# Whole-expert weight loads and a reordered expert loop in a two-block transformer kernel

## The chip, the cores and the metric

One Trainium2 chip, of which the kernel uses one core. The metric is device time in microseconds (us) for one execution. Everything is float32. TensorE (PE) multiplies, with its weight load shown apart as PEld; ScalarE is ACT, VectorE is DVE, GpSimd is POOL, SyncE is SP and issues most of the transfers.

## What is computed

Two models run one after the other on 256 tokens of width 1024. The first is two layers of attention, convolution and MLP. The second has two layers as well, and each of its layers ends in a mixture of experts. That is the part the change touches. Each token chooses one of four groups of experts and two of the eight experts in it:

```python
def _hier_moe(h, w_r1, b_r1, w_r2, b_r2, w_gate, w_up, w_down):
    ...
    eid = grp[:, None] * MOE_PER_GROUP + top_i
    combine = jnp.einsum('tk,tke->te', w_sel, jax.nn.one_hot(eid, MOE_EXPERTS, dtype=jnp.float32))

    def expert_step(acc, xs):
        wg, wu, wd, gcol = xs
        y = (jax.nn.silu(t @ wg) * (t @ wu)) @ wd
        return acc + y.astype(jnp.float32) * gcol[:, None], None
```

There are 32 experts per layer, each with three matrices of 1024 x 512 or 512 x 1024 (2 MB each, 6 MB per expert). The result of each expert is weighted and added into the tokens that chose it.

## The kernel before

The engines run programs written out by hand, and semaphores order them. All weights come from the chip's memory. Outside the experts they come in chunks of 2 MB (`CW` = 4096 floats in each of 128 partitions) into a ring of four slots (`ring`, `RING` = 4).

The expert stage is `moe(i)`, once per layer. After routing, it runs rounds (one round here: each expert gets at most 64 of the 256 tokens, `SLOTS`), and a round is eight **turns** of four experts (`TURNS`, `GROUP_OF`). In a turn:

- DVE builds `place` (which token goes to which slot) and `weighted` for four experts.
- PE **gathers** the tokens of all four experts at once (`gather`, 16 products of 128 x 256 into four PSUM banks), and ACT copies the four banks to `gathered`.
- Then for each of the four experts: `gate_up` (16 products, 128 x 512, which use two of the expert's three chunks), ACT's silu, DVE's product (`hidden`), `turn` (four transposes on PE, to bank 1), ACT's copy to `turned`, `down` (8 products with the third chunk) and DVE's copy to `y`. `spread` (8 products that add y to the tokens in the four `sums` banks) of an expert comes one expert later, between the next `gate_up` and the next `turn`. For the fourth expert it comes at the end of the turn.

On SP, `load_experts` issues a chunk as soon as the chunk four places earlier has been used: a third of an expert at a time, gated by `up_done` (the end of `gate_up`) or `down_done` (the end of `down`). So several transfers are in flight at most times:

```python
if t == 0:
    sp.wait_ge(S.sem(f"moe{i}_down_done"), it * 4 + (e + 1))
else:
    sp.wait_ge(S.sem(f"moe{i}_up_done"), it * 4 + (e + 2))
...
sp.dma_start(ring[:, q % RING, :], src).then_inc(S.sem(f"moe{i}_landed{q % RING}"), 16)
```

In the traces a float32 product is two matmul instructions, so `gate_up` shows as x32, `down`, `spread` and a quarter of a gather as x16, x16 and x8, `turn` as x4. Lines: L965 `gate_up`, L987 `down`, L996 `spread`, L494 `turn`, L473 `gather` (a helper that other stages use too), L1301 ACT's copy of gathered tokens, L1305 silu, L1307 ACT's copy to `turned`, L1964 `hidden`, L1967 the copy to `y`, L393 the issue of an expert chunk, L1011 the closing of `sums`.

Of the kernel before, what the change touches and what calls it, by code (L numbers as in the profile page):

```python
# [23 lines left out]
P = 128  # L24
T = 256
# [213 lines left out]
def two_blocks_kernel(nc, stream, experts, tokens, ctx_tokens, params, consts, consts2, pool_counts, positions,  # L239
                      na_bias, out, counted):  # L240
    stack = ExitStack()
    with stack:
# [37 lines left out]
        def carve(tensor, spec):  # L280
            at, views = 0, {}
            for name, *dims in spec:
                n = int(np.prod(dims))
                v = tensor[:, at:at + n]
                if len(dims) > 1:
# [24 lines left out]
                         ("weighted", 2, GROUP_OF * 2 * SLOTS), ("turned", 512), ("y", 512), ("silu", T), ("hidden", T)])  # L310
# [56 lines left out]
        def _(sp):  # L367
# [10 lines left out]
            def load_experts(i):  # L378

                S.wait(sp, "chunk_used", C_POOL - 1 if i == 0 else C_POOL)  # L380

                def turn(it, turn_no):
                    for q in range(EXPERT_CHUNKS * GROUP_OF):
                        e, t = q // EXPERT_CHUNKS, q % EXPERT_CHUNKS


                        if t == 0:
                            sp.wait_ge(S.sem(f"moe{i}_down_done"), it * 4 + (e + 1))
                        else:
                            sp.wait_ge(S.sem(f"moe{i}_up_done"), it * 4 + (e + 2))  # L390
                        n = i * EXPERTS * EXPERT_CHUNKS + q
                        src = experts[bass.ds(turn_no * 12 + n, 1), :, :].rearrange("a p c -> p (a c)")
                        sp.dma_start(ring[:, q % RING, :], src).then_inc(S.sem(f"moe{i}_landed{q % RING}"), 16)  # L393


                turn(0, 0)
# [38 lines left out]
        def _(pool):  # L435
# [6 lines left out]
            for i in range(2):  # L442
                for j, kind in enumerate(("down_done", "down_done", "up_done", "up_done")):
                    pool.memset(small[:, 120 + 4 * i + j:121 + 4 * i + j], 0.0).then_inc(S.sem(f"moe{i}_{kind}"), 1)

# [6 lines left out]
            S.wait(pool, "x_normed", "post", 0, 0)  # L452
# [6 lines left out]
        def _(pe):  # L459
# [450 lines left out]
            def moe(i):  # L910
# [29 lines left out]
                def landed(it, q):  # L940

                    raised(f"landed{q % RING}", it, 16 * (q // RING + 1), 48)
                    return ring[:, q % RING, :]

                def gather(it):

                    raised("placed", it, 1, 1)
                    for j in range(4):
                        bank = banks[3 - j]
                        for a in range(2):  # L950
                            k = 2 * j + a
                            mm = product(bank[:, a * T:(a + 1) * T],
                                         [(M["by_token"][:, t, k * P:(k + 1) * P], M["place"][:, t, :]) for t in range(2)])
                        give(mm, "gather_done")

                def gate_up(it, e):
# [3 lines left out]
                    for c in range(2):  # L960
                        w = landed(it, 3 * e + c).rearrange("p (k c) -> p k c", k=4)
                        for kk in range(4):
                            k = 4 * c + kk
                            for half in range(2):
                                mm = pe.matmul(banks[0][64 * half:64 * half + 64, :],  # L965
                                               M["gathered"][:, k, e * SLOTS:(e + 1) * SLOTS],
                                               w[:, kk, 512 * half:512 * half + 512], start=(k == 0), stop=(k == KT - 1))
                    give(mm, "up_done")

                def turn(it, e):  # L970
# [4 lines left out]
                    for t in range(2):  # L975
                        mm = transposed(banks[1][:, T + t * P:T + (t + 1) * P],
                                        M["weighted"][:, t, 2 * e * SLOTS:2 * (e + 1) * SLOTS])
                    give(mm, "turn_done")

                def down(it, e):  # L980

                    raised("turned", it, e + 1, 4)
                    w = landed(it, 3 * e + 2).rearrange("p (k c) -> p k c", k=4)
                    for k in range(4):
                        hT = M["turned"][:, (k % 2) * P + (k // 2) * 64:(k % 2) * P + (k // 2) * 64 + 64]
                        for half in range(2):
                            mm = pe.matmul(banks[2][64 * half:64 * half + 64, :], hT, w[:, k, 512 * half:512 * half + 512],  # L987
                                           start=(k == 0), stop=(k == 3))
                    give(mm, "down_done")

                def spread(it, e):

                    raised("y_kept", it, e + 1, 4)
                    for m in (0, 4, 1, 5, 2, 6, 3, 7):
                        a, c = 64 * (m // 4), (m % 4) * P
                        pe.matmul(sums[m // 2][:, (m % 2) * T:(m % 2 + 1) * T], M["y"][a:a + 64, c:c + P],  # L996
                                  M["turned"][a:a + 64, T:2 * T], start=False, stop=False, skip_group_check=True)

                with pe.Fori(0, rounds_of(pe, i)) as rnd:
                    with pe.Fori(0, TURNS) as g:  # L1000
                        it = rnd * TURNS + g
# [34 lines left out]
        def _(act):  # L1036
# [249 lines left out]
            def moe(i):  # L1286
# [9 lines left out]
                with act.Fori(0, rounds_of(act, i)) as rnd:  # L1296
                    with act.Fori(0, TURNS) as g:
                        it = rnd * TURNS + g
                        for j in range(4):
# [877 lines left out]
```

## Time and profile before

| | |
|---|---|
| device time, median of 3 runs | 2636.77 us (2635.98 to 2636.89) |
| the profiled execution, first to last instruction | 2643.5 us |
| PE busy | 2364.3 us (89%) |
| DVE, ACT busy | 909.9 us (34%), 480.3 us (18%) |
| read from memory | 619.08 MB, of which 192 expert chunks of 2 MB |
| expert stage of layer 0, first `gate_up` to the last `spread` | 1461.20 to 1979.42 us |
| expert stage of layer 1, the same | 2089.20 to 2607.08 us |

The profiled execution is read from the trace of one run, with times from its first instruction. The page gives for each engine its busy time; the chain of work is followed back from the last instruction to what released each step. PE counted as busy need not be PE at its peak, and a queue's time from issue to landing holds the waiting behind other transfers.

### The profile page before, as it was taken

The page shows a single profiled execution, that of the slowest core. Times are in us where ns is not written, and L with a number is a line of the kernel's source. Part 1 is how long each engine was busy: PE and PEld are TensorE (multiplying, and loading weights), DVE is VectorE, ACT ScalarE, POOL GpSimd, SP SyncE. Part 2 cuts the span into 40 slices and gives each one's busy share as a digit, 9 for nine tenths or more (in the row PEclk, how much of TensorE's full clock was granted, in tenths as well). Part 3 has the DMA queues.
Part 4 walks back from the last instruction along what each step waited for, and adds up shares of the span by engine and source line. Part 5 has one row for each costly group of instructions (what it writes and reads, how often), then busy time and mean ns, then how long its engine had stood idle before and what let it go on. Part 6 is the DMA issues. An engine that isn't in the chain of part 4 may idle for free.

```text
span 2643.5 us, 30301 instructions
## 1 busy us (share of the span) xinstructions
PE 2364.3 (89%) x12616; PEld 1594.5 (60%) x12616; DVE 909.9 (34%) x2001; ACT 480.3 (18%) x784; POOL 4.1 (0%) x20
## 2 busy tenths in 40 slices
PE   7999989989999899989887899999995799999996
PEld 6766779988767699946765344444433444444443
DVE  7889345541473365420364000000007300001002
ACT  1113113311221143210130111111110111111110
POOL 0000000000000000000000000000000000000000
PEclk9989999999999999999988999999997899999998
DMA  6335624534446434522003789999972399999993
GB/s 249 139 128 224 253 96 182 199 127 159 190 166 249 159 128 176 208 85 96 32 1 135 324 377 385 383 384 385 385 298 104 164 379 385 384 385 386 382 384 144
DMA packets 43320, 621.13 MB, mean 235 GB/s; under 512 B 4816, under 2 KB 4816, under 8 KB 5232
## 3 DMA queue, kind: packets, MB, share of 16 engines
q1 hardware_dynamic: 42624, 615.76, 57.1%
q0 software_dynamic: 624, 4.39, 0.4%
q8 instruction: 48, 0.79, 0.1%
q14 instruction: 24, 0.20, 0.0%
HBM read 619.08 MB, written 1.05 MB: 235 GB/s over the span
## 4 chain that ended last, share of the span: by engine, by line
PE 77%; DVE 11%; DMA 7%; ACT 3%; issue 1%; DVEq 0%; SPq 0%; ACTq 0%
PE bank L473 32%; PE bank L965 15%; DMA ring<-in_experts 7%; PE bank L987 6%; PE sums L996 3%; PE bank L656 2%; PE bank L657 2%; PE bank L658 2%; PE sums L658 2%; PE sums L657 2%; PE sums L656 2%; PE bank L494 2%; PE bank L483 2%; PE sums L717 2%; DVE wide L1433 1%; DVE arena L1460 1%
## 5 line engine op out<-in xcount | busy, mean ns | idle before, releaser
L965 PE MATMUL bank<-ring,wide 128*64 128x512 f32 x2048 | 455.2, 594 | 21.3 <-ACT wide L1301 12.2
L473 PE MATMUL bank<-h,ring 128*128 128x256 f32 x1920 | 440.1, 392 | 23.8 <-DVE h L1358 12.1
L473 PEld LDWEIGHTS bank<-h,ring 128*128 128x128 f32 x1920 | 375.2, 197 | 87.6 <-DVE h L1358 12.9
L965 PEld LDWEIGHTS bank<-ring,wide 128*64 128x64 f32 x2048 | 145.6, 137 | 314.9 <-issue 281.1
L987 PE MATMUL bank<-ring,wide 128*64 128x512 f32 x1024 | 233.8, 598 | 45.2 <-ACT wide L1307 45.2
L1964 DVE TENSOR_TENSOR wide<-bank,wide 128x256 f32<-128x256 f32 x64 | 27.2, 425 | 578.4 <-ACT wide L1305 578.4
L1660 DVE TENSOR_TENSOR ring_split<-ring,arena_split 128x2048 fp32r<-128x2048 f32 x64 | 143.8, 2288 | 110.6 <-ACT arena_split L1186 110.4
L473 PE MATMUL bank<-arena,ring 128*128 128x256 f32 x624 | 147.0, 398 | 31.9 <-DVE arena L1996 19.8
L1967 DVE COPY wide<-bank 128x512 f32<-128x512 f32 x64 | 44.3, 692 | 371.4 <-PE bank L987 371.4
L987 PEld LDWEIGHTS bank<-ring,wide 128*64 128x64 f32 x1024 | 68.3, 136 | 169.5 <-issue 125.1
L656 PE MATMUL bank<-h_split,arena_split 128*128 128x256 f32 x512 | 146.8, 287 | 15.0 <-DVE ring_split L1660 15.0
L473 PEld LDWEIGHTS bank<-arena,ring 128*128 128x128 f32 x624 | 124.2, 200 | 53.3 <-issue 15.5
L657 PE MATMUL bank<-scratch_split,arena_split 128*128 128x256 f32 x512 | 146.4, 286 | 0.0
L658 PE MATMUL bank<-h_split,ring_split 128*128 128x256 f32 x512 | 146.2, 286 | 0.0
L656 PE MATMUL sums<-smax_split,arena_split 128*128 128x256 f32 x512 | 144.9, 283 | 0.0
L657 PE MATMUL sums<-smax_split,arena_split 128*128 128x256 f32 x512 | 144.9, 283 | 0.0
L658 PE MATMUL sums<-smax_split,ring_split 128*128 128x256 f32 x512 | 144.9, 283 | 0.0
L1186 ACT ACTIVATE arena_split<-ring 128x2048 fp32r<-128x2048 f32 x64 | 118.9, 1906 | 113.3 <-PE sums L658 113.3
L996 PE MATMUL sums<-wide 64*128 64x256 f32 x1024 | 127.9, 389 | 12.7 <-DVE wide L1967 12.7
L996 PEld LDWEIGHTS sums<-wide 64*128 64x128 f32 x1024 | 93.6, 186 | 74.3 <-issue 38.9
L1305 ACT ACTIVATE wide<-bank 128x256 f32<-128x256 f32 x64 | 24.6, 384 | 619.4 <-PE bank L965 619.4
L473 PE MATMUL bank<-wide 128*128 128x256 f32 x528 | 124.3, 394 | 7.5 <-DVE wide L1952 7.5
(265 smaller groups left out, 2604.6 us busy)
## 6 DMA issues: line engine op xcount, KB each, us to landing
ring<-in_experts SPq DMA_DIRECT2D x192, 2048.0 KB, 12.4
ring<-in_stream SPq DMA_DIRECT2D x100, 2048.0 KB, 7.6
wide<-in_na_bias POOLq DMA_DIRECT2D x1, 1536.0 KB, 11.9
arena<-in_consts POOLq DMA_DIRECT2D x1, 1088.0 KB, 8.8
x<-in_tokens SPq DMA_DIRECT2D x1, 1024.0 KB, 6.2
scratch<-in_ctx_tokens POOLq DMA_DIRECT2D x1, 1024.0 KB, 5.0
out_x<-x SPq DMA_DIRECT2D x1, 1024.0 KB, 3.9
par<-in_params SPq DMA_DIRECT2D x1, 715.0 KB, 7.5
```

The costliest lines, as they stand in the source:

```text
L473: mm = pe.matmul(dst, a, b, start=(first and i == 0), stop=(i == len(terms) - 1))
L483: mm = pe.matmul(bank[:, 0:T], ones, src(0, q), start=(q == 0), stop=(q == tiles[0] - 1))
L494: return pe.transpose(dst, src, ident)
L656: pe.matmul(dst, w_hi, v_hi, start=start, stop=False, skip_group_check=True)
L657: pe.matmul(dst, w_hi, v_lo, start=False, stop=False, skip_group_check=True)
L658: return pe.matmul(dst, w_lo, v_hi, start=False, stop=stop, skip_group_check=True)
L717: mm = pe.matmul(sums[c % 2][g:g + 32, :], cond[:, k, :], w[:, k, :], start=(k < 4), stop=(k >= 4))
L965: mm = pe.matmul(banks[0][64 * half:64 * half + 64, :], M["gathered"][:, k, e * SLOTS:(e + 1) * SLOTS], w[:, kk, 512 * half:512 * half + 5 ...
L987: mm = pe.matmul(banks[2][64 * half:64 * half + 64, :], hT, w[:, k, 512 * half:512 * half + 512], start=(k == 0), stop=(k == 3))
L996: pe.matmul(sums[m // 2][:, (m % 2) * T:(m % 2 + 1) * T], M["y"][a:a + 64, c:c + P], M["turned"][a:a + 64, T:2 * T], start=False, stop=Fal ...
L1186: act.activation(HI[("up", "down")[part]][:, j % 2, :], ring[:, slot, 2048 * part:2048 * part + 2048], ACT.Copy).then_inc(S.sem("mlp_high" ...
L1660: dve.tensor_tensor(split["ring"][:, slot, 2048 * part:2048 * part + 2048], v, HI[("up", "down")[part]][:, j % 2, :].bitcast(F32), ALU.sub ...
```

## The change

The same products are computed. What differs:

1. **Weights.** An expert's three chunks lie side by side in memory (48 KB in each partition) and come in one transfer of 6 MB. There are two whole-expert buffers: the first three ring slots, and the first 12,288 columns of `arena`, a work area that is idle in the expert stages. The transfer of expert e waits until `down` of expert e-2 is done. The first two of a stage go out ahead.
2. **Order on PE.** The gather for the next turn is cut into four pieces, one in each expert, between `gate_up` and `turn`; only a round's first gather stands alone. Everything that belongs to gathered tokens has two buffers (`gathered`, `placed_at`, `weighted_at`; the second ones lie in `h` and `scratch`). `spread` of the previous expert moves from before `turn` to between `turn` and `down`, `turned` has two halves, and the first spread of a stage adds zeros. The loop over turns runs over pairs of turns, three times, and the last two turns are written out.
3. **ACT and DVE.** DVE instead of ACT copies the gathered tokens. DVE clears one half of `turned` and `y` ahead of the rounds.
4. **POOL.** The load of `pool_counts` (512 KB, into `arena`) waits for the end of layer 0's experts. Eight small memsets are gone.

```diff
             def load_experts(i):
-                S.wait(sp, "chunk_used", C_POOL - 1 if i == 0 else C_POOL)
-                def turn(it, turn_no):
-                    for q in range(EXPERT_CHUNKS * GROUP_OF):
-                        e, t = q // EXPERT_CHUNKS, q % EXPERT_CHUNKS
...
+                def turn(it, turn_no, first=False):
+                    for e in range(GROUP_OF):
+                        if first and i and e == 1:
+                            S.wait(sp, "chunk_used", C_POOL)
+                        if not first or e >= 2:
+                            sp.wait_ge(S.sem(f"moe{i}_down_done"), it * 4 + (e - 1))
+                        src = experts[bass.ds(turn_no * 4 + (i * EXPERTS + e), 1), :, :].rearrange("a p c -> p (a c)")
+                        sp.dma_start(expert_slots[e % 2], src).then_inc(S.sem(f"moe{i}_landed{e % 2}"), 16)
...
-            S.wait(pool, "x_normed", "post", 0, 0)
+            S.wait(pool, "moe_summed", 0)
             pool.dma_start(PL["counts"], pool_counts.rearrange("p (a b) -> p a b", a=4))\
...
-                        gather(it)
-                        for e in range(GROUP_OF):
-                            gate_up(it, e)
-                            if e:
-                                spread(it, e - 1)
-                            turn(it, e)
-                            down(it, e)
-                        spread(it, GROUP_OF - 1)
+                def experts_of(it, buf, last=False):
+                    for e in range(GROUP_OF):
+                        gate_up(it, e, buf)
+                        if not last:
+                            if e == 0:
+                                raised("placed", it, 2, 1)
+                            raised("gather_kept", it, 4 + e, 4)
+                            gather(1 - buf, e, banks[3])
+                        turn(it, e, buf)
+                        raised("y_kept", it, e + 1, 4)
+                        spread((e + 1) % 2)
+                        down(it, e)
...
-                        for j in range(4):
-                            act.wait_ge(S.sem(f"moe{i}_gather_done"), it * 4 + (j + 1))
-                            act.activation(flat2(M["gathered"][:, 2 * j:2 * j + 2, :]), banks[3 - j][:, :], ACT.Copy)\
-                               .then_inc(S.sem(f"moe{i}_gather_kept"), 1)
...
+                def keep_gathered(it, j, buf, bank):
+                    dve.wait_ge(S.sem(f"moe{i}_gather_done"), it * 4 + (j + 1))
+                    dve.tensor_copy(flat2(gathered[buf][:, 2 * j:2 * j + 2, :]), bank[:, :])\
+                       .then_inc(S.sem(f"moe{i}_gather_kept"), 1)
...
+                        dve.wait_ge(S.sem(f"moe{i}_silued"), it * 4 + (e + 1))
+                        dve.tensor_tensor(M["hidden"], banks[0][:, T:2 * T], M["silu"], ALU.mult)\
+                           .then_inc(S.sem(f"moe{i}_hidden"), 1)
+                        if not last:
+                            keep_gathered(it + 1, e, 1 - buf, banks[3])
+                        dve.wait_ge(S.sem(f"moe{i}_down_done"), it * 4 + (e + 1))
+                        dve.tensor_copy(M["y"], banks[2][:, :]).then_inc(S.sem(f"moe{i}_y_kept"), 1)
...
+                dve.memset(M["turned"][:, 1, :], 0.0)
+                dve.memset(M["y"], 0.0).then_inc(S.sem(f"moe{i}_y_kept"), 1)
```

**PE, two experts in the middle of a turn of layer 0.** The rows give line, operation, what is written and read, the shape, and the semaphores waited for. Before (L965 `gate_up`, L996 `spread`, L494 `turn`, L987 `down`; "landed" is the arrival of a chunk):

```order
L965 MATMUL bank<-ring,wide 64x512 [waits moe0_landed3]
L965 MATMUL bank<-ring,wide 64x512 x7
L935 REGISTER_ALU
L965 MATMUL bank<-ring,wide 64x512 [waits moe0_landed0]
L965 MATMUL bank<-ring,wide 64x512 x7
L996 MATMUL sums<-wide 128x256 [waits moe0_y_kept]
L996 MATMUL sums<-wide 128x256 x7
L935 REGISTER_ALU
L494 MATMUL bank<-con,wide 128x128 [waits moe0_hidden]
L494 MATMUL bank<-con,wide 128x128 x3
L987 MATMUL bank<-ring,wide 64x512 [waits moe0_landed1,moe0_turned]
L987 MATMUL bank<-ring,wide 64x512 x7
```

and of the changed kernel (L959 `gate_up`, L470 a piece of the gather, L491 `turn`, L989 `spread`, L981 `down`; "landed0" and "landed1" are the two whole-expert buffers):

```order
L959 MATMUL bank<-arena,wide 64x512 [waits moe0_landed1]
L959 MATMUL bank<-arena,wide 64x512 x7
L932 REGISTER_ALU
L470 MATMUL bank<-scratch,wide 128x256 [waits moe0_gather_kept]
L470 MATMUL bank<-scratch,wide 128x256 x3
L932 REGISTER_ALU
L491 MATMUL bank<-con,wide 128x128 [waits moe0_hidden]
L491 MATMUL bank<-con,wide 128x128 x3
L989 MATMUL sums<-wide 128x256 [waits moe0_y_kept]
L989 MATMUL sums<-wide 128x256 x7
L981 MATMUL bank<-arena,wide 64x512 [waits moe0_landed1,moe0_turned]
L981 MATMUL bank<-arena,wide 64x512 x7
```

A quarter of a gather now stands between `gate_up` and `turn`, `spread` stands between `turn` and `down`, and the wait of `down` for its own chunk is gone: what `gate_up` waited for holds all three matrices.

**SP, the first turn of layer 0's experts.** Before, 12 transfers, of which some wait for `up_done`:

```order
L376 DMA ring<-in_stream 128x4096 [waits filled] x5
L393 DMA ring<-in_experts 128x4096 [waits moe0_down_done,filled]
L393 DMA ring<-in_experts 128x4096 [waits moe0_up_done] x2
L393 DMA ring<-in_experts 128x4096 [waits moe0_down_done]
L393 DMA ring<-in_experts 128x4096 [waits moe0_up_done] x2
```

and of the changed kernel, 4 transfers:

```order
L382 DMA ring<-in_stream 128x4096 [waits filled] x5
L393 DMA ring<-in_experts 128x12288 [waits filled]
L393 DMA arena<-in_experts 128x12288
L393 DMA ring<-in_experts 128x12288 [waits moe0_down_done]
L393 DMA arena<-in_experts 128x12288 [waits moe0_down_done]
```

The first two have no wait for an expert, and each later one waits for `down_done` alone. No transfer starts at an `up_done` any more.

## Rows read from the trace of the kernel before

**Rows 1.** The page: the span, and the chain that ended last, by engine.

```profile
span 2643.5 us, 30301 instructions
...
PE 77%; DVE 11%; DMA 7%; ACT 3%; issue 1%; DVEq 0%; SPq 0%; ACTq 0%
```

**Rows 2.** Stretches: us, busy of PE, PEld, DVE, ACT, POOL, PEclk, DMA share, GB/s.

```profile
1461.20:1979.42 518.22, 471.71 (x2401) 209.18 (x2401) 49.55 (x93) 68.53 (x108) 0.00 (x0) 1.00 0.89 372
2089.20:2607.08 517.88, 471.73 (x2401) 209.36 (x2401) 49.56 (x93) 68.53 (x108) 0.00 (x0) 1.00 0.89 373
1585.44:1651.17 65.73, 59.82 (x306) 26.89 (x305) 6.43 (x13) 8.88 (x14) 0.00 (x0) 1.00 0.92 385
1470.00:1500.00 30.00, 27.32 (x142) 10.82 (x144) 2.23 (x4) 2.47 (x5) 0.00 (x0) 1.00 0.99 421
```

**Rows 3.** The chain in order of time, one turn: start us, us, what.

```profile
1585.44 7.12 PE bank L473 x32
...
1593.31 7.11 PE bank L965 x32
...
1606.33 6.87 PE bank L965 x32
1613.20 1.93 PE sums L996 x16
...
1620.05 6.89 PE bank L965 x32
...
1627.11 10.72 DMA ring<-in_experts
1637.83 0.04 issue
```

**Rows 4.** ACT in order of time, gathered copies: start us, us, what, idle before.

```profile
1587.40 0.60 ACT L1301 ACTIVATE wide<-bank 128x512 f32<-128x512 f32 x1 [7.16 <-PE bank L473]
1589.13 0.60 ACT L1301 ACTIVATE wide<-bank 128x512 f32<-128x512 f32 x1 [1.13 <-PE bank L473]
```

**Rows 5.** PE and SP in order of time: a `down`, the issue it releases.

```profile
1550.99 3.65 PE L987 MATMUL bank<-ring,wide 128*64 128x512 f32 x16 [0.69 <-ACT wide L1307]
...
1554.83 0.33 SPq L393 DMA_DIRECT2D ring<-in_experts  x1
```

**Rows 6.** Tiles `in_experts` (three issues by themselves), then `in_stream`: ns, starts, landing.

```profile
L393 SPq DMA_DIRECT2D ring<-in_experts x1: 327/327/327, 1406.4 to 1406.4; - x1
...
DMA to landing us min/median/max: 7.7/7.7/7.7
...
L393 SPq DMA_DIRECT2D ring<-in_experts x1: 676/676/676, 1407.7 to 1407.7; - x1
...
DMA to landing us min/median/max: 21.1/21.1/21.1
...
L393 SPq DMA_DIRECT2D ring<-in_experts x1: 328/328/328, 1468.3 to 1468.3; - x1
...
DMA to landing us min/median/max: 9.0/9.0/9.0
...
DMA to landing us min/median/max: 7.3/7.6/24.9
```

**Rows 7.** The chain: first `gate_up` of the last turn, in each stage.

```profile
1921.54 7.11 PE bank L965 x32
...
2549.00 7.11 PE bank L965 x32
```

**Rows 8.** DVE ahead of the first turn, and its memset by line: start, us.

```profile
1449.75 0.76 DVE L1952 TENSOR_TENSOR wide<-con,smax 128x256 f32<-128x256 f32 x2 [1.38 <-issue]
...
L1415 DVE MEMSET wide<- x1: 1765/1765/1765, 29.1 to 29.1; 128x2048 f32 x1
```

**Rows 9.** DMA issues (KB, us to landing), and DVE's first work in `arena` afterwards.

```profile
arena<-in_pool_counts POOLq DMA_DIRECT2D x1, 512.0 KB, 3.4
...
2013.95 0.29 DVE L1984 COPY arena<-h 128x256 f32<-128x256 f32 x1
```

More of the change, by code:

```diff
@@ L378, in load_experts @@
             def load_experts(i):
-                S.wait(sp, "chunk_used", C_POOL - 1 if i == 0 else C_POOL)
-                def turn(it, turn_no):
-                    for q in range(EXPERT_CHUNKS * GROUP_OF):
-                        e, t = q // EXPERT_CHUNKS, q % EXPERT_CHUNKS
[L387 to L396, printed above, removed]
+                def turn(it, turn_no, first=False):
[6 more added lines that the diff above has]
+                        sp.dma_start(expert_slots[e % 2], src).then_inc(S.sem(f"moe{i}_landed{e % 2}"), 16)
+                if i == 0:
+                    S.wait(sp, "chunk_used", C_POOL - 1)
+                turn(0, 0, first=True)
                 with sp.Fori(1, TURNS) as g:
@@ L938, in give, with landed, gather, gate_up @@
                     ins.then_inc(S.sem(f"moe{i}_{kind}"), 1)
[L940 to L947, printed above, removed]
-                    for j in range(4):
[L949 to L956, printed above, removed]
+                def landed(it, e, c):
+                    raised(f"landed{e % 2}", it, 16 * (e // 2 + 1), 32)
+                    return expert_slots[e % 2][:, c * CW:(c + 1) * CW]
+                def gather(buf, j, bank):
+                    for a in range(2):
+                        k = 2 * j + a
+                        mm = product(bank[:, a * T:(a + 1) * T],
+                                     [(M["by_token"][:, t, k * P:(k + 1) * P], placed_at[buf][:, t, :]) for t in range(2)])
+                    give(mm, "gather_done")
+                def gate_up(it, e, buf):
                     if e == 0:
@@ L960, in gate_up @@
                     for c in range(2):
-                        w = landed(it, 3 * e + c).rearrange("p (k c) -> p k c", k=4)
+                        w = landed(it, e, c).rearrange("p (k c) -> p k c", k=4)
                         for kk in range(4):
@@ L996, in spread @@
                         pe.matmul(sums[m // 2][:, (m % 2) * T:(m % 2 + 1) * T], M["y"][a:a + 64, c:c + P],
[L997 to L1001, printed above, removed]
-                        gather(it)
-                        for e in range(GROUP_OF):
-                            gate_up(it, e)
-                            if e:
-                                spread(it, e - 1)
-                            turn(it, e)
-                            down(it, e)
-                        spread(it, GROUP_OF - 1)
+                                  M["turned"][a:a + 64, before, T:2 * T], start=False, stop=False, skip_group_check=True)
+                def experts_of(it, buf, last=False):
[10 more added lines that the diff above has]
+                        down(it, e)
+                rounds = rounds_of(pe, i)
+                with pe.Fori(0, rounds) as rnd:
+                    raised("placed", rnd, 1, TURNS)
+                    for j in range(4):
+                        gather(0, j, banks[3 - j])
+                    with pe.Fori(0, TURNS // 2 - 1) as g:
+                        for b in range(2):
+                            experts_of(rnd * TURNS + g * 2 + b, b)
+                    experts_of(rnd * TURNS + (TURNS - 2), 0)
+                    experts_of(rnd * TURNS + (TURNS - 1), 1, last=True)
+                pe.wait_ge(S.sem(f"moe{i}_y_kept"), rounds * EXPERTS + 1)
+                spread(1)
                 for b in range(4):
@@ new lines, in moe @@
+                dve.memset(M["turned"][:, 1, :], 0.0)
+                dve.memset(M["y"], 0.0).then_inc(S.sem(f"moe{i}_y_kept"), 1)
+                with dve.Fori(0, rounds_of(dve, i)) as rnd:
+                    place(rnd * TURNS, 0, 0)
+                    for j in range(4):
+                        keep_gathered(rnd * TURNS, j, 0, banks[3 - j])
+                    with dve.Fori(0, TURNS // 2 - 1) as g:
+                        for b in range(2):
+                            experts_of(rnd * TURNS + g * 2 + b, g * 2 + b, b)
+                    experts_of(rnd * TURNS + (TURNS - 2), TURNS - 2, 0)
+                    experts_of(rnd * TURNS + (TURNS - 1), TURNS - 1, 1, last=True)
@@ L2095, in pack_experts @@
     out[:, :, 2] = a["moe_w_down_2"].reshape(2, EXPERTS, 4, P, D).transpose(0, 1, 3, 2, 4).reshape(2, EXPERTS, P, CW)
-    return out.reshape(2 * EXPERTS * EXPERT_CHUNKS, P, CW)
+    return out.transpose(0, 1, 3, 2, 4).reshape(2 * EXPERTS, P, EXPERT_CHUNKS * CW)
 def pack_params(a):
```

73 lines of the change are left out of this document (36 added, 37 removed).

## The prediction

> **What bounds the kernel now.** I read the page's span and chain first: PE holds 77% of the chain and transfers 7% [rows 1]. The change acts in the two expert stages alone, so I cut those out: 518.2 and 517.9 us, each at a granted clock of 1.00, with the transfers 0.89 busy and 372 to 373 GB/s [rows 2]. Both PE and memory are near their limit there, and the question is how they interlock. One turn takes 65.7 us at 385 GB/s, while a stretch in which chunks stood in the queue without a break moved 421 GB/s at a share of 0.99 [rows 2]. So transfers pause within a turn. The chain shows where: through the gather and the first `gate_up` PE leads, and late in the turn 10.7 us of a chunk's transfer are on the chain [rows 3]. All four slots stay full while PE gathers (7.12 us), no transfer runs, and the turn's last expert pays with a short wait. PE would have been ready for that chunk at 1620.05 + 13.72 (an expert, below) + 3.4 (half of 6.87) = 1637.2, and it landed at 1637.8 [rows 3]: PE alone needs only some 0.7 us less per turn. So hiding the gather from PE is worth something only if the transfers keep pace. That decides the case.
>
> **What the change does to PE.** From one `gate_up` to the next within a turn it is 13.72 us (1606.33 to 1620.05) [rows 3]: `gate_up`, `spread`, `turn`, a wait of 0.69 us for ACT's copy [rows 5], `down`. The new order adds a quarter of the gather, 1.73 us by the distance of two of ACT's copies [rows 4]. It puts `spread` (1.93 us [rows 3]) behind `turn`, which covers the 0.69 us of ACT. The quarter of the gather in turn covers silu and `hidden`, as `spread` did. That is 13.72 + 1.73 - 0.69 = 14.76 us, and 0.2 us more (7.11 against 6.87, less the part that is only the end of the last product [rows 3]) where `gate_up` starts after a wait: 14.96. Four experts are 59 to 60 us of PE per turn. If nothing else counted, a turn would lose 6 us.
>
> **What it does to the transfers.** A buffer is refilled only when its whole expert is done, so one buffer runs in a cycle: expert on PE, issue, transfer of 6 MB, next expert but one. The terms are 14.96 us of PE; 0.18 us from the end of `down` (1554.64) to SP's issue (1554.83) [rows 5]; the transfer T; 0.04 us from landing to PE [rows 3]. No row shows a transfer of 6 MB. The nearest are the four chunks issued back to back into an idle queue: the first, issued at 1406.4, landed after 7.7 us, the fourth, issued at 1407.7, after 21.1 [rows 6]. That is 14.7 us for three more, 4.9 us each, and three chunks, the same 6 MB, land 7.7 + 2 x 4.9 = 17.5 us after the first issue. I take T = 17.5. From below I bound it by the fastest chunk into an idle queue, 7.3 us, which gives 17.1; from above by the slowest of the expert chunks that met an idle queue, 9.0 us, which gives 18.8 [rows 6]. I stay near 17.5 since that is the same number of bytes from the same tensor.
>
> The cycle is 14.96 + 0.18 + 17.5 + 0.04 = 32.68 us for two experts, so 65.4 us per turn, against 65.7 of the one shown. The gather's 7 us vanish from PE's own sum, and a wait for a landing of about 3 us in every second expert takes their place. The fixed part of a transfer (7.7 - 4.9 = 2.8 us) was exposed once per turn, when the queue restarted after the gather; now it is exposed in each buffer's cycle.
>
> **The sum, per stage.** Seven turns at 65.36 are 457.5 us. The last turn has no gather left to hide, so a start after a wait costs 13.02 (first expert of a turn, 1593.31 to 1606.33 [rows 3]) - 0.69 + 1.93 = 14.26 us on PE. To the third expert: 14.26 + 0.18 + 17.5 + 0.04 = 31.98. Then 14.26 + 14.06, then 0.8 for the copy of y and 2.0 for the last `spread`: 63.1 us. At the start DVE clears two 128 x 512 areas, 0.44 us each (1.765 us for four times the size), but 1.38 us stand idle there while it loads the number of rounds [rows 8]; between nothing and 0.9 us, and DVE's copy costs about what ACT's did: I take 0.4. In all 521.0 us. Before, it was 518.2 and 517.9 us [rows 2]. The parts before tell where it goes: the first seven turns took 460.3 and 459.8 us, the last one 57.9 and 58.1 [rows 2, 7]. So seven turns gain 2.5 us and the last one loses 5.1, because its loads can no longer run ahead by single chunks. Both stages: 2.8 + 3.1 = +5.9 us. Against the profiled execution (2643.5 us) that is 2649.4; the median of the runs is 6.7 us under it (2636.8), and there it is 2642.7.
>
> **What costs nothing.** DVE gets four copies per turn of some 0.7 us; it works 6.4 us of 65.7 [rows 2] and its next task for PE comes at the end of the next `gate_up`. If that cover were gone, each copy would add 0.7 us. ACT loses four copies and a table load and waits anyway. `place` for the next turn runs under the first `gate_up`. The load of `pool_counts` moves from before the experts to about 1980; it took 3.4 us and is read at 2013.95 [rows 9]. It shares the engines with the C_POOL chunk and the first expert of layer 1, 8 MB or some 20 us, so even queued behind all of these it arrives at about 2005. It cannot hold up SP, since POOL issues it. If it were late, the pooling would start late by as much, once. PE waits for registers more often (the added `gather_kept`); 0.1 us for each expert exposed would add 0.1 per cycle, since an expert stands once in its buffer's cycle, 3 us in all.
>
> **What a unit is worth.** A stage has 15 such cycles, both have 30. Each 0.1 us in T or in an expert's PE time moves the kernel by 3 us. The forecast falls to no change at T = 17.3.
>
> The Trainium skill, DMA: Bandwidth & Descriptors, "Rules for kernel authors", asks for at least 1 MiB per transfer for full bandwidth, and to issue early so that the fixed setup overlaps. The 2 MB chunks fulfil both, so by it the size gains no rate and the lost overlap is a loss; the 4.9 us per 2 MB [rows 6] agree.
>
> **Rivals.**
> - *Faster: the transfer is short.* If one transfer saves what three issues cost, T comes to 17.1 or less and two buffers suffice. For it: the fastest lone chunk took 7.3 us. Against: the 4.9 us per 2 MB is nearly the pace of a full queue (421 GB/s), and one issue removes no byte. T = 17.1 gives 2642.7 - 12 = 2631. Under T = 17.3 it decides. Chance of under 2631.5: 20%, its upper edge just that.
> - The same skill page, "Anatomy of one DMA — SWDGE (gpsimd) path", fits 2.0 us + bytes / 436 GB/s, which would make T 16.4 us, an estimate, and the kernel 2610. By it a 2 MB chunk would take 6.8 us; the trace has 7.3 to 7.7, so I give this end 3% of the 20.
> - *No change: the interlock is as tight as before.* The cycle gains as much in the first seven turns as the last loses: T of 17.1 to 17.45, 2631.5 to 2642. For it: 65.4 and 65.7 us per turn are close. Chance 34%.
> - *Clearly slower: one engine's share is late each time.* A 6 MB transfer lands with the slowest of 16 engines, and nothing runs ahead of it. At 1468.3 a restart took 9.0 us in place of 7.7 [rows 6]. If rows of 48 KB add such a delay to each transfer, it is 30 x 1.3 = 39 us: 2682. Against: the issue at 1406.4 took 7.7, and the median of the stream's chunks is 7.6 [rows 6]. A partial case (0.4 to 0.8 us) gives 2655 to 2667. Chance of over 2655: 16%.
>
> **How the numbers follow.** A measurement of this kernel tells a change from none at about 0.2%, 5.3 us. The forecast case, T from 17.45 to 17.9, is 2642 to 2655, 30% (2642.7 is its likeliest point, as the step sum gives), no change 34%, faster 20%, clearly slower 16%. Slower is thus 46% in all, and likeliest. 2642.7 is rounded to 2643. The range reaches from T = 17.05 (2629) to T = 18.0 with 0.15 us more on PE per expert (2643 + 15 + 4.5 = 2662); this leaves out some 2 in 10. The range of the forecast's own case is 2642 to 2655.
>
> **What the profile after would show.** SP: two transfers of 6 MB ahead, then one after each `down`, and T as time to landing of about 17.5 us. The chain: `down` of an expert, transfer, `gate_up` two experts later, with no separate gather after the first; PE waits for a landing in every second expert, 2.5 to 3 us, or 1.3 in each. PE: 14.8 us from `gate_up` to the end of `down`. Turns of 65.4 us, the last of 63. The sum is wrong if T is off by more than 0.3 us, if the copy by DVE or `spread` ahead of `down` opens a new idle time on PE, or if the waits for a landing are absent; then PE sets the pace at 59 us and some 90 us are saved, which the 14.7 us that 6 MB need at full rate plus 2.8 us exclude as I read them.

## The result, and the profile after

The changed kernel takes **2705.9 us** (median of 4 runs, 2696.6 to 2714.6), against 2636.8 us before in the same comparison: a ratio of 1.0262, 95% interval 1.0233 to 1.0290. It is slower by 69 us. The forecast was 2643 with a range up to 2662, 6 us slower: the direction was right, the size was off by more than ten times.

The page of the kernel after, with the span, the chain by engine, the groups of `gate_up` (L959) and the issues of expert weights:

```profile
span 2707.3 us, 29921 instructions
...
PE 66%; DMA 20%; DVE 12%; ACT 1%; issue 1%; SPq 0%; DVEq 0%; ACTq 0%
...
L959 PE MATMUL bank<-ring,h 128*64 128x512 f32 x512 | 130.1, 667 | 39.7 <-DMA ring<-in_experts 39.7
L959 PE MATMUL bank<-ring,wide 128*64 128x512 f32 x512 | 131.6, 673 | 32.6 <-DMA ring<-in_experts 30.9
...
L959 PE MATMUL bank<-arena,h 128*64 128x512 f32 x512 | 123.6, 639 | 20.7 <-DMA arena<-in_experts 20.7
...
L959 PE MATMUL bank<-arena,wide 128*64 128x512 f32 x512 | 120.9, 627 | 14.8 <-DMA arena<-in_experts 14.6
...
ring<-in_experts SPq DMA_DIRECT2D x32, 6144.0 KB, 17.9
arena<-in_experts SPq DMA_DIRECT2D x32, 6144.0 KB, 18.9
```

Transfers went from 7% of the chain [rows 1] to 20%. Two things are to be read here. Of the idle time ahead of `gate_up`, 106 us end with a landing: that is the wait that was forecast. And a matmul instruction of `gate_up` takes 627 to 673 ns on average. That was not forecast; where the stage is at full clock (e3_land and e4_filler below) it is 592 to 595.

Windows of the kernel after: both expert stages (first `gate_up` to the last `spread`), then 3.41 us at the start of one `gate_up` that followed a wait, and 4.99 us behind them. The columns are those of [rows 2].

```profile
1452.22:2007.66 555.44, 495.82 (x2417) 215.16 (x2417) 68.79 (x121) 41.69 (x72) 0.00 (x0) 0.95 0.83 340
2117.79:2673.91 556.12, 500.51 (x2417) 216.47 (x2417) 68.90 (x121) 41.69 (x72) 0.00 (x0) 0.94 0.83 340
1484.60:1488.01 3.41, 3.12 (x8) 1.00 (x10) 0.00 (x0) 0.00 (x0) 0.00 (x0) 0.50 1.10 404
1488.01:1493.00 4.99, 4.99 (x26) 1.55 (x22) 0.00 (x0) 0.00 (x0) 0.00 (x0) 1.00 0.88 374
```

The stages grew by 37.2 and 38.3 us against [rows 2]. The transfers fell from 0.89 busy and 372 GB/s to 0.83 and 340, and the granted clock, 1.00 before in both stages, is 0.95 and 0.94. It is a mix of two levels: 0.50 (1.2 GHz) in the third row, 1.00 (2.4 GHz) in the fourth. Added up over the trace, 54.6 and 64.9 us of the stages are at half clock. Outside the stages the profiled execution was 11.6 us shorter than that of before (first `gate_up` at 1452.2 against 1461.2, and less at the end); e1_fine alone falls on either value (three executions at 2543 us, and the profiled one at 2552 with its first `gate_up` at 1462.1), so most of this is scatter between executions and not a gain.

The chain of the kernel after in order of time, three buffer cycles (start us, us, what):

```profile
1501.57 17.62 DMA ring<-in_experts
1519.19 0.04 issue
1519.23 8.52 PE bank L959 x32
1527.75 1.93 PE bank L470 x8
1529.67 0.44 PE bank L491 x4
1530.11 1.93 PE sums L989 x16
1532.04 3.61 PE bank L981 x16
...
1535.81 18.51 DMA ring<-in_experts
...
1554.36 7.09 PE bank L959 x32
1561.45 1.92 PE bank L470 x8
1563.38 0.44 PE bank L491 x4
1563.81 1.93 PE sums L989 x16
1565.74 3.61 PE bank L981 x16
...
1569.51 18.04 DMA ring<-in_experts
...
1587.59 8.47 PE bank L959 x32
```

This is the forecast cycle: an expert, the issue, the transfer, the same buffer again, with no separate gather. The second expert here takes 7.09 + 1.92 + 0.44 + 1.93 + 3.61 = 15.0 us, as predicted. The first and third start with 8.5 us of `gate_up`, 1.4 more, and the transfers take 17.6 to 18.5 us instead of 17.5. Averaged over the first seven turns of each stage, both buffers together, against the four terms of the prediction:

| us per cycle | predicted | layer 0 | layer 1 |
|---|---|---|---|
| expert on PE | 14.96 | 15.69 | 15.87 |
| `down` to the issue | 0.18 | 0.18 | 0.18 |
| transfer T | 17.5 | 18.63 | 18.46 |
| landing to PE (with buffers that landed before PE was free) | 0.04 | 0.30 | 0.46 |
| cycle | 32.68 | 34.79 | 34.97 |

The excess is 2.1 to 2.3 us per cycle, some 66 us in 30 cycles.

### The profile page after: what moved, and what is told of

It is laid out like the page before. It is cut to its first block, busy times and chain, and to the rows that moved or that the text cites. A ratio compares the mean times of both kernels' runs of the same rounds, so it can differ in the third digit from the quotient of the medians.

```text
span 2707.3 us, 29921 instructions
## 1 busy us (share of the span) xinstructions
PE 2399.3 (89%) x12648; PEld 1596.3 (59%) x12648; DVE 955.7 (35%) x2069; ACT 421.4 (16%) x704; POOL 3.9 (0%) x12
## 4 chain that ended last, share of the span: by engine, by line
PE 66%; DMA 20%; DVE 12%; ACT 1%; issue 1%; SPq 0%; DVEq 0%; ACTq 0%
PE bank L470 28%; DMA ring<-in_experts 13%; PE bank L959 11%; DMA arena<-in_experts 7%; PE bank L981 5%; PE sums L989 3%; PE bank L653 2%; PE bank L654 2%; PE bank L655 2%; PE sums L655 2%; PE sums L654 2%; PE sums L653 2%; DVE wide L1438 2%; PE bank L480 2%; DVE arena L1465 2%; PE bank L491 1%
## 5 line engine op out<-in xcount | busy, mean ns | idle before, releaser
L470 PE MATMUL bank<-h,ring 128*128 128x256 f32 x1920 | 431.5, 386 | 23.9 <-DVE h L1363 12.1
L470 PEld LDWEIGHTS bank<-h,ring 128*128 128x128 f32 x1920 | 369.2, 193 | 84.5 <-DVE h L1363 12.9
L470 PE MATMUL bank<-arena,ring 128*128 128x256 f32 x624 | 146.3, 397 | 31.8 <-DVE arena L2026 19.7
L959 PE MATMUL bank<-ring,h 128*64 128x512 f32 x512 | 130.1, 667 | 39.7 <-DMA ring<-in_experts 39.7
L959 PE MATMUL bank<-ring,wide 128*64 128x512 f32 x512 | 131.6, 673 | 32.6 <-DMA ring<-in_experts 30.9
L470 PEld LDWEIGHTS bank<-arena,ring 128*128 128x128 f32 x624 | 123.6, 200 | 53.0 <-issue 15.5
L959 PE MATMUL bank<-arena,h 128*64 128x512 f32 x512 | 123.6, 639 | 20.7 <-DMA arena<-in_experts 20.7
L959 PE MATMUL bank<-arena,wide 128*64 128x512 f32 x512 | 120.9, 627 | 14.8 <-DMA arena<-in_experts 14.6
L989 PE MATMUL sums<-wide 64*128 64x256 f32 x1056 | 131.8, 389 | 1.6 <-DVE wide L1985 1.6
L981 PE MATMUL bank<-ring,wide 128*64 128x512 f32 x512 | 116.9, 598 | 0.0
L981 PE MATMUL bank<-arena,wide 128*64 128x512 f32 x512 | 116.9, 598 | 0.0
```

Source lines behind the costliest of these rows:

```text
L470: mm = pe.matmul(dst, a, b, start=(first and i == 0), stop=(i == len(terms) - 1))
L959: mm = pe.matmul(banks[0][64 * half:64 * half + 64, :], gathered[buf][:, k, e * SLOTS:(e + 1) * SLOTS], w[:, kk, 512 * half:512 * half + 5 ...
L981: mm = pe.matmul(banks[2][64 * half:64 * half + 64, :], M["turned"][:, e % 2, at:at + 64], w[:, k, 512 * half:512 * half + 512], start=(k ...
```

## The experiments

**Theory A**: with whole-expert buffers the transfer is on the chain; it takes longer than assumed, and the waits for it make PE run at half clock afterwards. Rivals: the size of the transfer (B), or something in the new order. All kernels below but e8_weights are edits of the changed one.

**Transfer size alone: e2_three.** Three transfers of 2 MB, issued together when the whole buffer is free; PE waits for all three.

```diff
-sp.dma_start(expert_slots[e % 2], src).then_inc(S.sem(f"moe{i}_landed{e % 2}"), 16)
+for t in range(EXPERT_CHUNKS):
+    if t == 0 and (not first or e >= 2):
+        sp.wait_ge(S.sem(f"moe{i}_down_done"), it * 4 + (e - 1))
+    sp.dma_start(expert_slots[e % 2][:, t * CW:(t + 1) * CW], src[:, t * CW:(t + 1) * CW])\
+      .then_inc(S.sem(f"moe{i}_landed{e % 2}_{t}"), 16)
```

> The changed kernel with each expert's 6 MB issued as three transfers of 2 MB (same rows in memory, same two buffers, same release at the end of down, and PE still waits for all three before gate_up). Theory A (the loss is two waits per pair of experts: one buffer's refill starts only at the end of its expert and PE idles about 3 us, after which the granted clock falls for 3.4 us; the size of a transfer does not matter): a load of the three takes 17.5 to 18 us when it meets an idle queue and 19 when it overlaps, half-clock stretches stay in about every second expert, 2690 to 2720 us. Rival B (rows of 48 KB in one transfer are slow): the load falls to 17.5 us everywhere, 2640 to 2670 us.

Measured 2702.5 us (2690.3 to 2709.6), 1.0238 (1.0204 to 1.0273). That is the changed kernel's time. An expert's three chunks together take 17.6 us from the first issue to the last landing when nothing was in flight and 19.0 when something was, and 20 `gate_up`s ran in part at half clock. Its first expert stage:

```profile
1457.22:2005.68 548.46, 484.72 (x2417) 223.37 (x2417) 68.69 (x121) 41.69 (x72) 0.00 (x0) 0.98 0.85 344
```

So it isn't the 6 MB in one piece, nor the row of 48 KB; rival B is out.

**The clock: e4_filler.** After each expert's `down` PE does two more products that nobody reads (1.5 us), to fill part of the wait.

```diff
                         down(it, e)
+                        if not last:
+                            raised("gather_kept", it, 5 + e, 4)
+                        for n in (512, 256):
+                            pe.matmul(banks[3][:, 0:n], S_zero, con[:, 0:n], start=True, stop=True)
```

> The changed kernel with two extra products per expert (zeros times a constant, 512 and 256 columns, into the free bank 3) right after down, 1.3 us of PE work that is thrown away and that falls into the idle time before a landing. Theory A (idle PE lowers the granted clock, and the half-clock stretch costs 1.6 us or 3.0 us of the next gate_up): no half-clock stretch inside the expert stages, gate_up 7.1 us throughout, pair of experts 33 us in place of 34.7, 2645 to 2665 us, that is 40 to 60 us faster than the changed kernel with more work on PE. Rival C (the clock falls for another reason, such as the load on memory or the new order of products): stretches stay, 2700 to 2740 us.

Measured 2683.0 us (2675.8 to 2685.8), 1.0181 (1.0164 to 1.0198): 23 us less than the changed kernel with more work on PE. Both stages:

```profile
1452.49:1991.51 539.02, 520.59 (x2545) 230.52 (x2545) 68.81 (x121) 41.69 (x72) 0.00 (x0) 1.00 0.86 350
2097.59:2637.78 540.19, 520.76 (x2545) 230.53 (x2545) 68.90 (x121) 41.69 (x72) 0.00 (x0) 1.00 0.85 350
```

The granted clock is 1.00 and both stages are 16 us shorter. The expert on PE is 14.96 us, the predicted term. The cycle, 33.7 us, is that, 0.18, a T of 18.2 to 18.4, and 0.3 of waiting after the landing. So without the half-clock stretches the profiled stages are 32 us shorter (23 us in the medians; the two profiled executions lie at opposite ends of their ranges). That is less than the 40 to 60 I expected, and it is what remains after the filler's own cost: where PE did not wait, the filler is on the chain.

```profile
1517.12 1.49 PE bank L1008 x4
```

With it two experts need 32.8 us of PE instead of 29.5. The price of the clock alone is therefore at least this; how much more was not measured. Of what is left, T is the larger part.

**Two transfers at once: e9_serial.** In the changed kernel 26 transfers were issued after the previous one had landed and took 17.86 us on average. The other 34 were issued while it was still in flight, by 2 to 4 us mostly, and took 19.0 us, up to 19.9. This kernel issues a transfer only after the first product of the expert ahead, that is after the previous landing.

```diff
-    sp.wait_ge(S.sem(f"moe{i}_down_done"), it * 4 + (e - 1))
+    sp.wait_ge(S.sem(f"moe{i}_begun"), it * 4 + e)
...
+    if k == 0 and half == 0:          # gate_up's first product
+        give(mm, "begun")
```

> The changed kernel, whole-expert buffers and one transfer of 6 MB per expert, but a transfer is issued only once the next expert's first product has run, that is after the previous transfer has landed, so no two transfers of experts are ever in flight together. In the changed kernel the transfers issued while the previous one was still in flight landed after 19.0 us on average, the others after 17.9. Theory A (two transfers that share the engines make each other late): all transfers now land after 17.5 to 18.0 us. The transfers follow each other with 0.6 us for the product, 0.2 for the issue and 0.04 between, 18.6 us per expert, 37.2 per pair instead of 34.7: 30 x 2.5 = 75 us more, about 2780 us. Theory B (a 6 MB transfer scatters between 17.5 and 19.9 us by itself): the mean stays at 18.5 with single ones up to 19.9, 38.6 us per pair, about 2820 us. A third reading, in which the memory pipe was starved by the wait for an expert and fewer waits would help, would give no more than 2706 us; I exclude it, since here transfers alone set the pace.

Measured 2833.4 us (2830.6 to 2838.2), 1.0757 (1.0739 to 1.0775), above both expected times. T alone answers the question. The issues and the chain:

```profile
ring<-in_experts SPq DMA_DIRECT2D x32, 6144.0 KB, 17.9
arena<-in_experts SPq DMA_DIRECT2D x32, 6144.0 KB, 17.6
```
```profile
1568.17 1.96 PE bank L959 x3
...
1570.28 17.53 DMA arena<-in_experts
...
1587.85 1.17 PE bank L959 x3
...
1589.18 18.17 DMA ring<-in_experts
```

The 60 transfers that waited for `begun` took 17.8 us on average, and four of them more than 18.5 (19.1 at most). So T is 17.8 by itself, and 1.2 us more when it starts in the tail of another: theory A of this run. Why they get in each other's way was not tested. The time is 53 us above its estimate; 47 of these come from the step that gates the issue, which takes 0.9 to 2.0 us, 1.39 on average, not the 0.6 that I had put down (a float32 product is two instructions, and in about half of the experts they ran in a half-clock stretch).

**The new order alone: e6_ring4.** The order of the changed kernel, with the ring of four 2 MB slots and the releases of before.

```diff
+for t in range(EXPERT_CHUNKS):
+    q = e * EXPERT_CHUNKS + t
+    if not first or q >= RING:
+        if t == 0:
+            sp.wait_ge(S.sem(f"moe{i}_down_done"), it * 4 + (e - 1))
+        elif t == 1:
+            sp.wait_ge(S.sem(f"moe{i}_up_done"), it * 4 + e)
+    sp.dma_start(ring[:, q % RING, :], src[:, t * CW:(t + 1) * CW])\
+      .then_inc(S.sem(f"moe{i}_landed{q % RING}"), 16)
```

> The new order on PE, DVE and ACT alone: the weights come as before, in 2 MB chunks through the ring of four slots, each chunk issued when the chunk four places earlier is used. Theory A (the loss sits in the whole-expert buffers, the new order is a gain): a turn falls from 65.7 us to what limits then, PE's 14.8 us per expert (59.1) or memory's 12 x 4.9 (58.8), 59 to 60 us per turn, clock 1.00 in the stage, 2540 to 2560 us. Rival D (the new order itself costs, through DVE's copies, through the change of product shape ahead of down, or through the clock): 2640 us or more.

Measured **2551.7 us** (2549.7 to 2553.9), 0.9682 (0.9666 to 0.9698): 85 us faster than before. Both stages:

```profile
1453.06:1926.31 473.25, 467.71 (x2417) 211.43 (x2417) 68.80 (x121) 41.69 (x72) 0.00 (x0) 1.00 0.96 408
2036.70:2510.26 473.56, 467.71 (x2417) 211.44 (x2417) 68.89 (x121) 41.69 (x72) 0.00 (x0) 1.00 0.96 408
```

PE is busy 99% of the stage, at full clock, and the transfers keep up at 408 GB/s. The first seven turns take 412.75 us, 58.96 each, against 65.7.

**The buffers alone: e8_weights.** The order of before, with whole-expert buffers and one transfer of 6 MB (and the later load of `pool_counts`, since `arena` is now a buffer).

```diff
+    for e in range(GROUP_OF):
...
+            sp.wait_ge(S.sem(f"moe{i}_down_done"), it * 4 + (e + 1))
...
+        sp.dma_start(expert_slots[e % 2], src).then_inc(S.sem(f"moe{i}_landed{e % 2}"), 16)
...
-    raised(f"landed{q % RING}", it, 16 * (q // RING + 1), 48)
-    return ring[:, q % RING, :]
+    e, c = q // 3, q % 3
+    raised(f"landed{e % 2}", it, 16 * (e // 2 + 1), 32)
+    return expert_slots[e % 2][:, c * CW:(c + 1) * CW]
```

> The weights part alone: the order of the kernel before on all engines, with whole-expert transfers of 6 MB into the two buffers, released at the end of down. Theory A: the cycle of a buffer is 13.9 + 0.2 + 17.5 to 18, PE waits about 4 us at the third expert of each turn and the queue's restart is on the path, 69 to 71 us per turn against 65.6, with half-clock stretches after the long waits: 2690 to 2740 us. If the whole-expert buffers harmed only together with the new order: 2640 to 2660 us.

Measured 2732.9 us (2728.1 to 2740.5), 1.0370 (1.0340 to 1.0400). Of its page the groups of `gate_up`, and a window around the start of one that followed a wait:

```profile
L962 PE MATMUL bank<-ring,wide 128*64 128x512 f32 x1024 | 260.6, 667 | 80.0 <-DMA ring<-in_experts 67.8
...
L962 PE MATMUL bank<-arena,wide 128*64 128x512 f32 x1024 | 225.2, 592 | 0.6 <-DMA arena<-in_experts 0.6
```
```profile
1481.68:1488.51 6.83, 5.17 (x12) 1.45 (x14) 0.00 (x0) 0.00 (x0) 0.00 (x0) 0.50 1.07 461
```

In layer 0 the third expert of each turn waits about 4 us for a ring buffer and then runs `gate_up` in 9.3 to 9.6 us; the buffers in `arena` do neither. So the loss comes with the buffers, whatever the order. The four kernels together:

| | ring of four 2 MB slots | whole-expert buffers |
|---|---|---|
| old order | 2636.5 | 2732.9 (+96) |
| new order | 2551.7 (-85) | 2705.9 (+69) |

The two parts do not add: -85 and +96 would give +11. With the ring PE sets the pace once the order is new, and the order is worth 85 us. With whole-expert buffers the buffer's cycle sets it, and the same order is worth 27 us (2732.9 to 2705.9).

**Which half of the wholeness costs: e1_fine, e3_land, e7_rel.** All keep the two large buffers. e3_land issues three transfers when the whole buffer is free, but PE waits for each third by itself. e7_rel frees and issues by thirds, but PE waits for all three. e1_fine does both by thirds. Its edit:

```diff
+for t in range(EXPERT_CHUNKS):
+    if not first or e >= 2:
+        kind = "down_done" if t == 2 else "up_done"
+        if t != 1:                    # thirds 0 and 1 go at up_done
+            sp.wait_ge(S.sem(f"moe{i}_{kind}"), it * 4 + (e - 1))
...
-raised(f"landed{e % 2}", it, 16 * (e // 2 + 1), 32)
+raised(f"landed{e % 2}_{c}", it, 16 * (e // 2 + 1), 32)
```

e3_land has the second half of this, with the wait for `down_done` of e2_three ahead of its three issues; e7_rel has the first half, and ahead of `gate_up`:

```diff
+for t in range(EXPERT_CHUNKS):
+    raised(f"landed{e % 2}_{t}", it, 16 * (e // 2 + 1), 32)
```

> The changed kernel with both buffers, but handled by thirds: each 2 MB third has a transfer and a landing of its own, and is refilled as soon as it is used (the two of gate_up at the end of gate_up, the one of down at the end of down). Six thirds in place of the ring's four slots. Theory A: 59 to 60 us per turn, no half-clock stretch, 2540 to 2560 us, and against the ring of four slots no difference or at most a few us, since both are near memory's pace of 4.9 us per 2 MB. Rival D (the order costs): 2640 us or more.

> The changed kernel with three transfers of 2 MB per expert into the same two buffers; release stays whole (all three wait for the end of down), and PE waits for each third by itself. Theory A: from the end of down the first third lands after 7.7 us and the second after 12.6, so gate_up starts 5 to 10 us earlier than with a whole landing and only the third's landing at 17.5 us has to meet down, 11 us later; the buffer's cycle falls under PE's own 29.5 us per pair, PE sets the pace at 59 us per turn, clock 1.00, 2540 to 2560 us. If the release of whole buffers were what costs, it would stay over 2640 us.

> The other half: each third is refilled as soon as it is used, but PE waits until all three have landed before gate_up. Theory A: two thirds are issued 8 us before the end of down, and the last one needs 7.7 us after it if the queue is free, so the cycle is 15.0 + 0.2 + 7.7 = 23 us, again under PE's 29.5 per pair: 2540 to 2565 us. Either half of the granularity is then enough. If landing by thirds were what matters, it would stay over 2640 us.

Measured: e1_fine **2543.5 us** (2542.6 to 2552.2), 0.9647 (0.9631 to 0.9663); e3_land **2542.9 us** (2542.4 to 2545.3), 0.9643 (0.9623 to 0.9664); e7_rel 2552.0 us (2551.5 to 2554.8), 0.9675 (0.9655 to 0.9695). The first stage of e3_land, then of e7_rel:

```profile
1452.92:1924.54 471.62, 467.05 (x2417) 211.72 (x2417) 68.80 (x121) 41.63 (x72) 0.00 (x0) 1.00 0.95 401
```
```profile
1461.58:1933.20 471.62, 467.05 (x2417) 212.09 (x2417) 68.70 (x121) 41.63 (x72) 0.00 (x0) 1.00 0.95 401
```

Both are 471.62 us, and e1_fine's is 471.61. Either half is enough: a release at `up_done` goes out some 8 us before `down` ends, and a start on the first third doesn't wait for the other two; each takes several us off a cycle that was 5.3 to 5.5 us longer than the 29.5 us that PE needs for two experts. PE then sets the pace. The 9 us between e7_rel and e3_land lie outside the stages, ahead of the first `gate_up` (1461.58 against 1452.92), as in the one slower execution of e1_fine; what they are was not tested. e3_land and e1_fine are the fastest versions found, 93 us under the kernel before.

**Where `spread` stands: e5_early.** e1_fine with `spread` back ahead of `turn`.

```diff
-                        turn(it, e, buf)
                         raised("y_kept", it, e + 1, 4)
                         spread((e + 1) % 2)
+                        turn(it, e, buf)
                         down(it, e)
```

> The kernel with the buffers handled by thirds, which PE bounds, with spread put back ahead of turn (the order of the kernel before, the gather still in quarters). Theory A: ACT's copy to turned lies open again, 0.69 us in each of 64 experts, 44 us in all, 2580 to 2595 us. A rival in which the change of product shape from spread to down costs as much as the copy: no change, 2540 to 2550 us.

Measured 2594.6 us (2590.9 to 2597.5), 0.9834 (0.9810 to 0.9857), 51 us above e1_fine. PE in order of time, with the idle time before each piece in brackets:

```profile
1532.60 2.00 PE L993 MATMUL sums<-wide 64*128 64x256 f32 x16
1534.53 0.44 PE L495 MATMUL bank<-con,wide 128*128 128x128 f32 x2
...
1535.87 1.51 PE L985 MATMUL bank<-ring,wide 128*64 128x512 f32 x6 [0.69 <-ACT wide L1315]
```

The 0.69 us ahead of `down` are back. From one `gate_up` to the next it is 15.65 us in the first seven turns of a stage instead of 14.74 in e1_fine: 0.91 us, of which 0.69 are the wait. The other 0.22 us lie in how the pieces join; on the chain `turn` takes 0.60 us there instead of 0.44 and `down` 3.65 instead of 3.58. So the wait of 0.69 us was read rightly, the place of `spread` is worth 0.2 us more than that, and 51 of the 93 us hang on it.

## Why the prediction was wrong

- **PE's sum**: right at full clock, in part by luck. 14.96 us per expert behind a wait were predicted, and e4_filler has 14.96; 14.76 from one `gate_up` to the next, and e1_fine has 14.74. But two terms were each off by 0.2 us, and the errors cancel: a quarter of the gather adds 1.93 us to the chain, not 1.73, and `spread` behind `turn` saves 0.91, not 0.69 (e5_early, which has the gather's quarter and not the move, takes 13.72 + 1.93 = 15.65). The copy by DVE, `spread` ahead of `down` and the later `pool_counts` opened no wait on PE.
- **Where the transfers pause in the kernel before**: read wrongly. "All four slots stay full while PE gathers (7.12 us), no transfer runs" does not hold. In the gather of the turn shown, and in the `gate_up` behind it:

```profile
1585.44:1593.31 7.87, 7.11 (x34) 5.93 (x33) 0.04 (x1) 2.50 (x5) 0.00 (x0) 1.00 1.00 427
1593.31:1600.40 7.09, 7.09 (x32) 2.28 (x32) 0.00 (x0) 1.17 (x1) 0.00 (x0) 1.00 0.32 134
```

  The slots fill during the gather, at 427 GB/s, and the queue runs dry in the first `gate_up`. The pause is there once per turn, one step later than the prediction has it, and no term of its sum changes.
- **The cycle**: right in form. The chain has its four links, and 0.18 and 0.04 us are as read.
- **The step that failed**: "a wait for a landing of about 3 us in every second expert takes their place" priced the wait and nothing behind it; the 14.96 us were taken with the granted clock of [rows 2], where PE never waits so long. After such a wait PE ran at 1.2 GHz for 3.41 or 6.83 us, and `gate_up` took 8.5 to 10.1 us instead of 7.1, in 28 of 60 experts. The 28 `gate_up`s together took 53.5 us longer than they do at full clock. Of this e4_filler gives back 32 us in the profiled stages, 23 in the medians, after the cost of its filler. The prediction had no term and no rival for it. The Trainium skill has it, in TensorE: Matmul & The Clock Gate, "HAM oscillation — how this bites in real kernels": a wait for a transfer ahead of each tile sends PE back to half clock, and half of the throttled time is lost. The trace agrees on the pattern (28 of 30 long waits), and on the half for PE's own work: of the 119.5 us at half clock in the stages 109 lie within these `gate_up`s, and 53.5 us are lost there; the other 11 lie in the waits, where they cost nothing. Half of all 119.5 us, 60 us, is more than the 23 to 32 that the kernel got back. One reason is the filler's own cost, another the coupling of the two buffers, told next.
- **The term that was mis-sized**: T. 17.5 us were taken. Alone a 6 MB transfer takes 17.8 (e9_serial), and 19.0 when it starts before the previous one has landed. The mean is 18.5, so one us in each of 30 cycles: 30 us, which by the prediction's own unit gives 2673. That was within its bound of 18.8 for T and beyond its range, which stopped at 18.0. The prediction put the two buffers' cycles side by side as if they didn't touch; 14.96 + 0.18 < 17.5 says that two transfers must overlap by some 2.5 us, and I didn't price that. The rival "one engine's share is late each time" (16%) had this size, but for another reason, the row length; e2_three, with rows of 16 KB and the same time, speaks against that one.
- **The two errors overlap.** In layer 1 of the changed kernel the buffer whose expert waited has 16.9 us on PE and a T of 17.8; the other has 14.9 us and a T of 19.0, and lands 0.8 us before PE is free. There the first buffer sets the pace, and its excess is nearly all clock. Without the half-clock stretches (e4_filler) the long T comes onto the chain, 19.45 us at 1533.68 for one. So what each error costs by itself is not a fixed share of the 70 us.
- **The last turn** was put at 63.1 us and took 71.0 and 68.4: the same two errors, and in layer 0 a wait of 3.9 us ahead of the fourth expert, where none was put.
- **The sum**: 37 us of the stages' 70 us over the forecast are left without the half-clock stretches (e4_filler: 539.0 and 540.2 against 521.0). There T is 0.8 us above its value, 24 us in 30 cycles, the buffers that landed before PE was free (it is at the filler then) add 0.24 us per cycle, 7 us, and the rest is in the last turns.
- **What the prediction gave away**: "If nothing else counted, a turn would lose 6 us." It would: 6.8 us per turn in e6_ring4. The claim that PE at 59 us per turn is excluded held only for whole-expert buffers.

The change thus holds two edits of opposite sign. The order hides the gather and ACT's copy, worth 85 us where the weights keep up. The buffers put a whole transfer into a cycle with a whole expert: 14.96 + 0.18 + 17.8 + 0.04 = 33.0 us at the least, over the 29.5 us that PE needs for two experts.

## What to carry to other kernels

For a double-buffered load, add one tile's compute, the issue and one transfer, and compare with the compute of two tiles; if the first is larger, the excess is a wait in every cycle, and freeing or landing the buffer in parts removes it. Price such a wait on PE with what follows it: look in the trace whether PE has ever waited that long at full clock, and if it hasn't, add a stretch at half clock. When a change joins two edits, run each alone: here a gain of 85 us was hidden under a loss, and the two did not add.

## What the hardware showed

- Of the waits of PE ahead of `gate_up` in the changed kernel, 30 lasted 2.64 to 4.86 us, and 28 of them had a stretch at a granted clock of 0.50 behind or at their end; two (2.93 and 3.50 us) had none. In e4_filler none of 22 waits from 0.52 to 1.99 us had one. Between 2.0 and 2.6 us the changed kernel has two waits, without one. The length of the wait alone does not decide it: in e2_three waits from 2.51 us on had a stretch behind them, and seven of 2.6 to 3.3 us had none; in e8_weights one of 3.91 us had none.
- Of two transfers of 6 MB that overlap by 2 to 4 us, the one that starts in the other's tail takes 1.2 us longer than alone, and its 16 completions are spread over 2.07 us instead of 1.5, on average.
- A filler of 1.5 us on PE behind each expert, whose result nobody reads, made a kernel that waits for transfers 23 us faster.
